# Recurrence and final projection in one block, with seven heads' products of two token tiles ahead of the last head's transposes

## What is computed

```python
def rec_out(o, z, gnorm, w_out, dtype):
    B, L = o.shape[:2]
    o = o * lax.rsqrt(jnp.mean(o * o, axis=-1, keepdims=True) + EPS) * gnorm.astype(jnp.float32)
    o = o.reshape(B, L, REC_WIDTH) * jax.nn.silu(z.astype(jnp.float32))
    return o.astype(dtype) @ w_out
...
        h = h + out
    y_prompt = rmsnorm(h, final_norm_w)
```

## Time and profile before

| | before |
|---|---|
| median of 3 runs | 1458.36 us (1457.74 to 1459.96) |
| the profiled execution, its own time | 1460.28 us |
| its span, first to last instruction | 1458.5 us |
| granted TensorE clock, mean | 0.982 |
| TensorE busy | 1382.0 us (95%), 8028 matmuls |
| VectorE busy | 927.7 us (64%) |
| ScalarE busy | 640.3 us (44%) |
| GpSimd busy | 553.8 us (38%) |

### The profile page before, as it was taken

The page is one execution under the profiler, slowest core; times in us unless marked ns, Lnnn a source line. Parts: engine busy times, 40 slices in busy tenths (PEclk is TensorE's granted clock), DMA queues, the critical chain, the costliest instruction groups (busy, mean ns, idle before and its releaser), DMA issues. The chain is left out here.

```text
span 1458.5 us, 21147 instructions
## 1 busy us (share of the span) xinstructions
PE 1382.0 (95%) x8028; PEld 1204.3 (83%) x8028; DVE 927.7 (64%) x1702; ACT 640.3 (44%) x1123; POOL 553.8 (38%) x399
## 2 busy tenths in 40 slices
PE   5999999999995899999998999999999999997998
PEld 5999845999993455548888999999999999996786
DVE  4211287878887988744557676767585858596233
ACT  4333365667765555541124534343443435343121
POOL 2466600455641001100023655556464737373000
PEclk9999999999997999999999999999999999998999
DMA  7221100223211400002221101111111111105221
GB/s 217 91 56 44 44 1 1 65 81 99 71 40 59 159 15 19 0 30 84 90 78 46 44 25 55 36 44 35 44 35 45 35 44 35 45 6 209 101 87 65
DMA packets 95315, 86.80 MB, mean 60 GB/s; under 512 B 5584, under 2 KB 83280, under 8 KB 95216
## 3 DMA queue, kind: packets, MB, share of 16 engines
q1 hardware_dynamic: 93584, 80.63, 18.0%
q0 software_dynamic: 1632, 4.82, 0.9%
HBM read 65.46 MB, written 19.97 MB: 59 GB/s over the span
## 5 line engine op out<-in xcount | busy, mean ns | idle before, releaser
L187 PE MATMUL bank<-hn_hi,rw_hi 128*128 128x352 f32 x768 | 251.7, 328 | 1.6 <-DVE hn_lo L177 1.6
L187 PE MATMUL bank<-hn_hi,rw_lo 128*128 128x352 f32 x768 | 247.9, 323 | 0.0
L187 PE MATMUL bank<-hn_lo,rw_hi 128*128 128x352 f32 x768 | 247.6, 322 | 0.0
L187 PE MATMUL bank<-hn_hi,w_hi 128*128 128x352 f32 x648 | 209.9, 324 | 0.0
L187 PE MATMUL bank<-hn_lo,w_hi 128*128 128x352 f32 x648 | 207.8, 321 | 0.0
L187 PE MATMUL bank<-hn_hi,w_lo 128*128 128x352 f32 x648 | 207.7, 321 | 0.0
L187 PEld LDWEIGHTS bank<-hn_hi,rw_hi 128*128 128x128 f32 x768 | 145.1, 189 | 3.5 <-issue 3.0
L187 PEld LDWEIGHTS bank<-hn_lo,rw_hi 128*128 128x128 f32 x768 | 145.6, 190 | 0.0
L187 PEld LDWEIGHTS bank<-hn_hi,rw_lo 128*128 128x128 f32 x768 | 145.2, 189 | 0.0
L721 POOL TENSOR_TENSOR swapped<-swapped,sin 128x352 f32<-128x352 f32 x57 | 54.0, 947 | 190.8 <-ACT swapped L668 125.8
L187 PEld LDWEIGHTS bank<-hn_hi,w_hi 128*128 128x128 f32 x648 | 121.6, 188 | 0.5 <-ACT relu L682 0.5
(11 more groups left out here) (230 smaller groups left out, 2926.1 us busy)
## 6 DMA issues: line engine op xcount, KB each, us to landing
rw_raw<-in_rec_w_in SPq DMA_DIRECT2D x32, 512.0 KB, 4.0
w_raw<-in_att_w_in SPq DMA_DIRECT2D x27, 512.0 KB, 4.0
q_rotated<-relu SPq DMA_DIRECT2D x24, 176.0 KB, 1.9
xin<-in_x_prompt SPq DMA_DIRECT2D x8, 512.0 KB, 3.8
q_tile<-q_rotated SPq DMA_DIRECT2D x8, 512.0 KB, 3.9
wo_raw<-in_att_w_out SPq DMA_DIRECT2D x4, 1024.0 KB, 9.2
x_again<-in_x_prompt SPq DMA_DIRECT2D x8, 512.0 KB, 4.1
residual<-h_rows SPq DMA_DIRECT2D x8, 512.0 KB, 2.9
```

The source lines that it names most:

```text
L187: last = pe.matmul(out, l, r, start=n == 0, stop=n == len(passes) - 1)
```

## The change

It does five things.

1. `out_recur_final` puts `final_out` in the same block as the recurrence; the join between them is gone, and so are the functions' own blocks.
2. The split tiles `f_hi` and `f_lo` move from `final_out` to `recurrence` and lie over buffers of the recurrence that are dead by then: tile 0's over `logs` and `b`, tile 1's over `kb` and `kbT`. The rest of `final_out`'s buffers lie over `levels`.
3. For tiles 0 and 1 the split is made in two steps: heads 0 to 6 early, head 7 late. The early ones stand on ScalarE between the second and third weight piece, and on VectorE ahead of `wf_lo` piece 2; the late ones at the end of the recurrence.
4. TensorE does the early part (21 products, left 512 columns) of tiles 0 and 1 ahead of head 7's `out_T`, in banks 0 and 2, and only the last 3 products of those two halves afterwards. The other halves stay whole.
5. The stored heads come back in nine DMAs, one for each tile, the first two between the weight pieces, and the residual's first loads wait for the last `out` product in place of the join.

```diff
-            sp.wait_ge(acc_ready, RH * PER_HEAD)
-            for c, (ks, cols) in enumerate(weight_pieces()):
-                sp.dma_start(S["wf_raw"][:, ks, cols], w_final[:, ks, cols]).then_inc(wf_in[c], 16)
-            sp.wait_ge(g_stored, 16 * STORED)
-            sp.dma_start(S["gT"][:, 0:STORED, :], g_dram[0:STORED].rearrange("h p t -> p h t")).then_inc(g_in, 16)
-            sp.wait_ge(g_in, 16)
+            def load_gated(t):
+                sp.dma_start(S["gT"][:, 0:STORED, span(t)],
+                             g_dram[0:STORED, :, span(t)].rearrange("h p t -> p h t")).then_inc(g_in[t], 16)
+
+            sp.wait_ge(acc_ready, RH * PER_HEAD)
+            load_weights(0)
+            load_weights(1)
+            sp.wait_ge(g_stored, 16 * STORED)
+            load_gated(0)
+            load_gated(1)
+            load_weights(2)
+            load_weights(3)
+            for t in range(2, NT):
+                load_gated(t)
...
+    def final_hi(act, t, late):
+        of = f_heads(t, late)
+        act.wait_ge(dve_read, n_dve[at["out_T", RH - 1 if late else RH - 2, 2, None] + 1])
+        act.wait_ge(g_in[t], 16)
+        if t >= 2:
+            act.wait_ge(final_ready, 2 * (t - 1))
+        act.copy(f_hi[t % 2][:, of], S["gT"][:, of, token_block(t)[0]]).then_inc(f_hi_done, 1)
...
+    def final_product(pe, t, n, heads):
+
+        w_n = [x[:, :, n * 512:(n + 1) * 512] for x in (S["wf_hi"], S["wf_lo"])]
+        if (t, n) in ((0, 0), (0, 1)):
+            pe.wait_ge(wf_lo_dve if n else wf_lo_pool, 2)
+        pe.wait_ge(f_lo_done, f_count(t, heads.stop == RH))
+        for k in range(heads.start, heads.stop):
+            for x, y in ((f_hi, 0), (f_lo, 0), (f_hi, 1)):
+                last = pe.matmul(ps[(2 * t + n) % 4][:], x[t % 2][:, k, :], w_n[y][:, k, :],
+                                 start=k == 0 and x is f_hi and y == 0, stop=k == RH - 1 and y == 1)
+        return last
...
+            pe.wait_ge(acc_read, RH * PER_HEAD)
+            for t in range(2):
+                final_product(pe, t, 0, slice(0, EARLY))
             for g in range(3):
                 multiply("out_T", RH - 1, g)
...
-                    for c in range(3):
+                    for c in range(2):
                         final_weights_hi(c)
+                    final_hi(act, 0, False)
+                    act.wait_ge(product_ready, at["state", RH - 1, 2, None] + 1)
+                    final_hi(act, 1, False)
+                    final_weights_hi(2)
                 for g in range(3):
                     read_product("out", p, g, o)
             final_weights_hi(3)
+            for t in range(2):
+                final_hi(act, t, True)
...
-            final_weights_lo(dve, 2)
+            for t in range(2):
+                final_lo(dve, t, False)
+            final_weights_lo(dve, 2, wf_lo_dve)
             norm_sums(RH - 1)
             norm(RH - 1)
-            final_weights_lo(dve, 3)
+            final_weights_lo(dve, 3, wf_lo_dve)
             gate_out(RH - 1)
+            for t in range(2):
+                final_lo(dve, t, True)
```

`final_lo` is the same on VectorE, with a wait for `final_hi`'s count. `EARLY` is 7. In `final_out` TensorE's stream is, for each tile t and half n:

```diff
+                u = 2 * t + n
+                if u >= 4:
+                    pe.wait_ge(h_ready, u - 3)
+                final_product(pe, t, n, slice(S["EARLY"] if t < 2 and n == 0 else 0, RH)).then_inc(out_ready, 1)
```

More of the change, by code:

```diff
@@ L1853, in final_out @@
     io, sem, ps = S["io"], S["sem"], S["ps"]
[L1854 to L1857, removed]
+    stats, half = S["stats"], S["half"]
+    final_hi, final_lo, final_product, out_ready = (S[n] for n in ("final_hi", "final_lo", "final_product", "final_ready"))
@@ L1858, in final_out @@
+    fw_in, h_in, shifted = sem("fw_in"), [sem("h_in0"), sem("h_in1")], sem("sample_rows2")
+    h_ready, squares_ready = sem("h2_ready"), sem("sq2")
     mean_ready, rstd_ready, y_ready, stored = sem("mean2"), sem("rstd2"), sem("y_ready"), [sem("y_stored0"), sem("y_stored1")]
[L1859 to L1862, removed]
+    space = Space(nc, S["levels_at"])
@@ L1863, in final_out, with sync @@
     rows_s = space("sample_rows_f", [DEC, D])
     fw = space("final_w", [P, D])
-    h = space("h_again", [P, 3, D])
+    h = space("h_again", [P, 2, D])
     y = space("y", [P, 2, D])
     junk = space("junk2", [P, D])
[L1868 to L1887, removed]
+    def sync(sp):
+        S["wait_h_stored"](sp)
+        sp.wait_ge(*S["products_done"])
+        sp.dma_start(fw[:], io["final_norm_w"].partition_broadcast(P)).then_inc(fw_in, 16)
+        for t in range(NT):
+            if t >= 2:
+                sp.wait_ge(y_ready, t - 1)
+                sp.wait_ge(squares_ready, t - 1)
+            sp.dma_start(h[0:rows(t), t % 2, :], S["h_dram"][span(t), :]).then_inc(h_in[t % 2], 16)
+            if t >= 1:
+                sp.wait_ge(y_ready, t)
+                sp.dma_start(y_rows(io, t - 1), y[0:rows(t - 1), (t - 1) % 2, :]).then_inc(stored[(t - 1) % 2], 16)
+        sp.wait_ge(y_ready, NT)
+        sp.dma_start(y_rows(io, SAMPLE), y[0:DEC, SAMPLE % 2, :]).then_inc(stored[SAMPLE % 2], 16)
+        sp.wait_ge(stored[0], 16 * ((NT + 1) // 2))
+        sp.wait_ge(stored[1], 16 * (NT // 2))
@@ L1888, in _, with scalar @@
+    def scalar(act):
+        for t in range(NT):
+            r = rows(t)
+            if 2 <= t + 1 < NT:
+                final_hi(act, t + 1, True)
+            if t == SAMPLE:
                 for n in range(2):
                     u = 2 * t + n
[L1890 to L1923, removed]
@@ L1948, in _ @@
-        @block.gpsimd
-        def _(pool):
-            for t in range(NT):
-                norm_stats_pool(pool, stats, half, t, squares_ready, t + 1, mean_ready, rstd_ready)
+                    act.wait_ge(out_ready, u + 1)
+                    act.copy(rows_s[:, n * 512:(n + 1) * 512], ps[u % 4][token_block(t)[1], :]).then_inc(shifted, 1)
+            act.wait_ge(h_ready, 2 * t + 2)
+            if t:
+                act.wait_ge(squares_ready, t)
+            act.activation(junk[0:r], h[0:r, t % 2, :], ACT.Square,
+                           accum_out=stats[0:r, 0, t:t + 1]).then_inc(squares_ready, 1)
@@ L1954, in y_rows, with gpsimd @@
+    def gpsimd(pool):
+        for t in range(NT):
+            norm_stats_pool(pool, stats, half, t, squares_ready, t + 1, mean_ready, rstd_ready)
+    return dict(sync=sync, tensor=tensor, scalar=scalar, gpsimd=gpsimd, vector=vector)
 def y_rows(io, t):
```

103 lines of the change are left out of this document (65 added, 38 removed).

## The result

The changed kernel takes 1449.72 us in the median of four runs (1448.71 to 1450.37), against 1458.85 us of before in the same session (1457.74 to 1459.96). The ratio is 0.9937, with a 95% interval of 0.9925 to 0.9949: 9.1 us faster, where 13.3 us had been forecast. The forecast of 1445.1 us lies under the result, and so does its range of 1443.0 to 1449.0, by 0.7 us at its upper end.

The account below looks back on a forecast made before the run. TensorE's waits, final products and tail were taken to bound the kernel. 9.5 + 1.2 + 1.6 + 88.4 + 0.2 = 100.9 us in place of 114.2, 13.3 less, gave 1445.1 us from the 1458.36 median; range 1443.0 to 1449.0.

Parts of the forecast that it names:

- Parts 1 and 2: Behind the last `out` product: 42 early products without a wait, 9.5 us, then nine transposes at 1.21 us instead of 2.18.
- rivals C and D: Loads before the early products: C, inputs late, about 1449 us, chance 0.04; D, ScalarE held up, 1462.7 us, chance 0.04.
- Part 4: The late products: 390 at 0.2267 us, 88.4 us plus 0.2 for the end, the new pass order priced at nothing.
- a pace over 0.23 us: Sign in the late products that the forecast was wrong: it would mean the order of the passes is not free.
- Part 3: Between transposes and late products: a gap of 1.6 us for head 7's gates, cast and subtraction, bounds 1.2 to 2.4.
- Rival B: Clock falls in the gap before the late products, costing 2.5 to 2.7 us: 1447.7 us, chance 0.12.

Follow-up runs that it names:

- late_loads: Changed kernel with all four weight pieces loaded ahead of the nine stored-head loads; 104.4 us from last `out` product to last final product.
- old_passes: Changed kernel with the three passes in the order of before; 102.7 us from last `out` product to last final product.
- same_again: Changed kernel run again with nothing edited; median of six runs 1450.66 us, ratio 0.9936 to before.
- again_2: Changed kernel run once more with nothing edited, for another profile; 1449.05 us in one run.
- again_3: Changed kernel run once more with nothing edited, for another profile; 1448.31 us in one run.
- swapped: Changed kernel with the places of even and odd split tiles exchanged; 102.5 us from last `out` product to last final product.
- the shifts: Kernel with the filled gap, tile 0's parts begun 128 or 256 bytes later; median 1444.06 us (ratio 0.9897) with 128, 1446.97 us in one run with 256.
- no_early: Changed kernel with the 42 early products moved from ahead of the transposes to behind them; median 1455.46 us, ratio 0.9971 to before.
- the filled gap: Changed kernel with 21 more products (heads 0 to 6, tile 0's right half) behind the transposes; median 1446.85 us, ratio 0.9908 to before.

## Why the prediction was too low

**Parts 1 and 2 (the early products and the transposes) held.** 42 products stand where TensorE idled, they start without a wait, the transposes find `o_rec` ready and take 1.22 us at the full clock, and nothing that was moved on ScalarE, VectorE or SyncE came late. `late_loads` shows that rivals C and D were farther away than thought. From the end of the last `out` product to the transposes it was 9.67 us rather than 9.5; the first half of the early products is tile 0's, and slow.

**Part 4's step on the pace failed.** "The new order of the three passes I price at nothing" was right, as `old_passes` shows. But the forecast took the pace of before, 0.2267 us, for all 390 late products, 88.6 us in all, and gave no thought to the operands' new place. Without the clock's fall they took 90.0 us (`same_again`, `again_2`, `again_3`). Tile 0's starts 128 bytes off a multiple of 256, and each of the five even tiles costs 0.27 us more: 1.35 us in all. The forecast's sign for this, a pace over 0.23 us, was there (0.2323 in the even tiles), but it named the order of the passes as the cause, and so would have blamed the wrong edit; `swapped` and the shifts give the right one.

**Part 3's gap was 1.9 us and not 1.6.** It lay in its bounds of 1.2 to 2.4. The steps between engines took more than the 0.1 us allowed for them: the gates began 0.74 us after the transposes rather than 0.6, and the first late product 0.44 us after the subtraction's start, where 0.28 had been set.

**Rival B was real, and its chance too small.** It had 0.12 and came in three of eight profiles. Its price was set at 2.5 to 2.7 us, from the earlier trace rows, where the low clock had lasted 5.5 us of products; behind this gap it lasts 3.4 us and costs 1.6. It was argued away by the gap's being shorter than those that had brought a fall. But each of those was one execution. The fall came 1.8 us into the wait for `o_rec` in the first profile of before, 3.7 us in the second and 5.0 us in `no_early`, and the gap of 1.8 us without a fall was one execution too: the same gap brings the fall or doesn't.

**The baseline.** The profile of before that the sum was made against had a stretch 0.7 us longer than a second one. Against the mean of the two, 113.8 us, the changed kernel's stretch is shorter by 9.5 us with the fall and 11.1 without; weighted by the seven profiles of kernels with the gap and the slow place (two with the fall), by 10.6 us. The interval of the first ratio is 7.4 to 10.9 us, which holds this. Of the 13.3 us forecast, 1.35 went to the place, 0.3 to the gap, 0.1 to the step from the last `out` product to the first early one, 0.45 to the clock on average and 0.35 to the baseline's mean; some 0.1 more is spread over small steps. What is left between 10.6 and the measured 9.1 us is not explained by any row. It lies outside the stretch, whose start scatters by almost 5 us, and stays open. The result lay 0.7 us above the range. Either the 1.35 us of the pace or the unexplained 1.5 us is more than that, so the miss of the range is in part bad luck; the wrong pace is a fault of the working in any case.

**The best version** here is the one with the filled gap and the shift of 128 bytes: 99.4 us of stretch, every product at the pace of before and at the full clock, and 15 us under before.

## What to carry to other kernels

When a change gives a matmul's operands a new place in SBUF, the pace per matmul is a term to price anew, even if shapes and types stay; an alternation of the pace from tile to tile, without idle time, points to the places, and exchanging two places settles it in one run. Work moved ahead of a wait is worth that wait only up to the next one: look at once for more work that is ready for the gap that is left, since in the three profiles with the gap filled the clock's fall behind it was gone as well. And one and the same short gap can bring the low clock in some executions and not in others, so one profile doesn't price it.

## What was not expected of the hardware

- Matmuls of float32r with 512 columns ran at 0.2323 us each when the 128 by 128 operand's buffer started at an odd multiple of 128 bytes (11.15 us for 48), and at 0.2267 when it started at a multiple of 256 (10.88 us), counted from a common base. The evidence is the three starts of tile 0's parts (shifts of 0 and 256 bytes slow, of 128 bytes fast) and the exchange of the two places. Only the 128 by 128 operand was moved; what in its reading is slowed, and whether the start of the weights matters too, is open.
- The clock fell after TensorE had taken up work again: with the gap ending at 1349.86, the granted clock was 1.00 until about 1350.9 and 0.50 from there to 1354.3. Behind gaps of the same 1.9 us it did so in three profiles of eight.
- Within the wait for `o_rec` the clock fell after 1.8 us in one profile of before, after 3.7 us in the other and after 5.0 us in `no_early`. The products behind it then ran at 0.50 for 5.5, 4.0 and 2.1 us.
- The wait for `o_rec` of 7.16 us and the gap of 4.0 us (two profiles) and the gap of 1.9 us (eight) repeat from execution to execution to 0.02 us, while the time at which the stretch begins scatters by almost 5 us.
